# Hybrid decoder trunk on one core: the silu gates of attention, convolution and scan made by ScalarE's Silu function

## What is computed

```python
def hybrid_layer(x, ...):
    h = rms_norm(x, norm_g)
    u = h @ w_in
    c_q, c_kv, k_pe, g_mla, u_conv, g_conv, z, xbc, dt_raw = jnp.split(u, offs, axis=-1)
    o_mla = mla_mixer(c_q, c_kv, k_pe, ...) * jax.nn.silu(g_mla)        # 6 heads x 128
    o_conv = conformer_conv_mixer(u_conv, ...) * jax.nn.silu(g_conv)    # 512 wide, 31 taps, layer norm, silu, @ w_pw
    o_ssd = ssd_mixer(z, xbc, dt_raw, ...)                              # 768 wide, rms_norm(y * silu(z), norm_g)
    y = jnp.concatenate([o_mla, o_conv, o_ssd], axis=-1) @ w_out
    return x + y
```

## Time and profile before

| what | value |
|---|---|
| time, median of 3 runs | 1636.02 us (1632.85 to 1638.46) |
| the profiled execution's own time | 1634.22 us |
| its span, first to last instruction | 1632.4 us |
| TensorE matmul busy | 1555.7 us (95%) |
| VectorE busy | 1066.7 us (65%) |
| ScalarE busy | 615.6 us (38%) |
| mean granted TensorE clock | 0.985 of full speed |
| moved by DMA | 158.13 MB, 97 GB/s |

### The profile page before, as it was taken

How to read it: one execution, slowest core, us unless ns; L and a number is a source line. 1 busy time by engine, 2 the same in 40 slices (tenths; PEclk the granted TensorE clock), 3 DMA queues, 4 the chain that set the end, 5 groups by cost and what they waited for, 6 DMA issues and landing times.

```text
span 1632.4 us, 18535 instructions
## 1 busy us (share of the span) xinstructions
PE 1555.7 (95%) x7062; PEld 1238.4 (76%) x7062; DVE 1066.7 (65%) x1738; ACT 615.6 (38%) x855; POOL 44.6 (3%) x86
## 2 busy tenths in 40 slices
PE   6999999999988999999999999899999799999997
PEld 5877776777776777888877877677778678778886
DVE  6545764889999876543455457758999996773221
ACT  6444453334333344212244355433443334352120
POOL 0000000000000000101000000000000000001100
PEclk9999999999998999999999999999999999999999
DMA  5322221222222323444422223121112233225442
GB/s 214 96 94 78 91 80 63 66 68 73 75 94 84 106 76 100 145 139 155 136 96 75 89 82 100 65 78 65 65 65 98 77 102 102 77 91 167 142 142 65
DMA packets 44423, 158.13 MB, mean 97 GB/s; under 512 B 5520, under 2 KB 5808, under 8 KB 44336
## 3 DMA queue, kind: packets, MB, share of 16 engines
q1 hardware_dynamic: 36720, 129.64, 24.4%
q0 software_dynamic: 6464, 23.12, 5.0%
q10 hardware_dynamic: 1152, 4.19, 0.7%
HBM read 148.50 MB, written 8.44 MB: 96 GB/s over the span
## 4 chain that ended last, share of the span: by engine, by line
PE 69%; DVE 19%; ACT 7%; issue 3%; DMA 1%; DVEq 0%; SPq 0%; POOL 0%; ACTq 0%; POOLq 0%
PE acc L489 14%; PE acc L491 14%; PE acc L490 14%; PE S L489 4%; PE S L490 4%; PE S L491 4%; PE S L494 3%; DVE wlo L986 3%; ACT whi L740 3%; DVE xb L977 3%; DVE cacc L1034 3%; PE T L490 2%; PE T L491 2%; PE T L489 2%; DVE xg L968 1%
## 5 line engine op out<-in xcount | busy, mean ns | idle before, releaser
L489 PE MATMUL acc<-hhi,whi 128*128 128x512 f32 (+1 forms) x1504 | 604.9, 402 | 23.1 <-DVE wlo L986 23.1
L986 DVE TENSOR_TENSOR wlo<-stage,whi 128x1024 fp32r<-128x1024 f32 (+3 forms) x252 | 300.4, 1196 | 451.9 <-ACT whi L740 449.9
L491 PE MATMUL acc<-hhi,wlo 128*128 128x512 f32 (+1 forms) x1504 | 590.5, 393 | 0.0
L490 PE MATMUL acc<-hlo,whi 128*128 128x512 f32 (+1 forms) x1504 | 589.8, 392 | 0.0
L740 ACT ACTIVATE whi<-stage 128x1024 fp32r<-128x1024 f32 (+3 forms) x252 | 259.6, 1035 | 467.3 <-PE acc L491 249.3
L489 PEld LDWEIGHTS acc<-hhi,whi 128*128 128x128 f32 (+1 forms) x1504 | 284.4, 189 | 87.1 <-DVE wlo L986 25.1
L490 PEld LDWEIGHTS acc<-hlo,whi 128*128 128x128 f32 (+1 forms) x1504 | 284.4, 189 | 61.9 <-issue 3.6
L491 PEld LDWEIGHTS acc<-hhi,wlo 128*128 128x128 f32 (+1 forms) x1504 | 283.4, 188 | 62.7
L1034 DVE SCALAR_TENSOR_TENSOR cacc<-glu,pv,cacc 128x512 f32<-128x512 f32 x240 | 171.8, 748 | 4.6
L489 PE MATMUL S<-hhi,whi 128*128 128x512 f32 x192 | 75.5, 393 | 0.0
L728 ACT ACTIVATE prob<-S,cols 128x128 f32<-128x128 f32 (+3 forms) x48 | 25.4, 529 | 131.7 <-DVE cols L972 131.7
(11 more groups left out here) (228 smaller groups left out, 1601.0 us busy)
## 6 DMA issues: line engine op xcount, KB each, us to landing
stage<-weights SPq DMA_DIRECT2D x236, 512.0 KB, 3.4
y_features<-xg POOLq DMA_DIRECT2D x32, 256.0 KB, 4.2
acsb<-acs_rows POOLq DMA_DIRECT2D x16, 384.0 KB, 4.2
xg<-x_features ACTq DMA_DIRECT2D x8, 512.0 KB, 11.4
xr<-x_features POOLq DMA_DIRECT2D x16, 256.0 KB, 4.2
xr<-y_features POOLq DMA_DIRECT2D x16, 256.0 KB, 4.0
stage<-weights SPq DMA_DIRECT2D x8, 256.0 KB, 2.9
stage<-weights SPq DMA_DIRECT2D x4, 384.0 KB, 3.0
```

Of the source, the lines that this page charges most:

```text
L489: nc.tensor.matmul(out, a, c, start=start, stop=False)
L490: nc.tensor.matmul(out, a, d, start=False, stop=False)
L491: return nc.tensor.matmul(out, b, c, start=False, stop=stop)
L986: nc.vector.tensor_tensor(wlo[u % RING][:, 0:w], stage[u % STAGE][:, 0:w], whi[u % RING][:, 0:w].bitcast(F32), ALU.subtract).then_inc(lo_d ...
```

## The change

For gmla, gconv and z, VectorE evicts without the factor 0.5; ScalarE runs Silu on temp and writes the gate itself, into xg for gmla and gconv, into temp2 for z; VectorE's silu() is replaced by gated(), which puts the tap as before and waits for tanh_done, and for z the product reads temp2. ug, xbc and the layer norm's silu stay as they were. The diff:

```diff
@@ -806,8 +806,13 @@
-                        if kind in ("gmla", "ug", "gconv", "z"):
+                        if kind == "ug":
                             tanh()
+                        if kind in ("gmla", "gconv", "z"):
+                            tanhs[0] += 1
+                            gate = temp2[:, :] if kind == "z" else xg[:, i if kind == "gmla" else 6 + i, :]
+                            act.wait_ge(tanh_in.sem, tanh_in.at(layer, tanhs[0]))
+                            a(tanh_done, gate, temp[:, :], ACT.Silu)
@@ -996,6 +1001,13 @@
+                def gated():
+
+                    if taps_open[0]:
+                        convolve(1)
+                    tanhs[0] += 1
+                    dve.wait_ge(tanh_done.sem, tanh_done.at(layer, tanhs[0]))
+
@@ -1142,14 +1154,14 @@
-                            evac(j, temp[:, :], half=True)
+                            evac(j, temp[:, :])
                             mark(tanh_in)
-                            silu(None, xg[:, i if kind == "gmla" else 6 + i, :], temp[:, :])
+                            gated()
                         elif kind == "z":
-                            evac(j, temp[:, :], half=True)
+                            evac(j, temp[:, :])
                             mark(tanh_in)
-                            silu(None, temp[:, :], temp[:, :])
-                            tt(None, xg[:, 10 + i, :], xg[:, 10 + i, :], temp[:, :], ALU.mult)
+                            gated()
+                            tt(None, xg[:, 10 + i, :], xg[:, 10 + i, :], temp2[:, :], ALU.mult)
```

## The result

The changed kernel takes **1627.05 us** (median of 5 runs, 1624.6 to 1629.92) against 1636.02 us (1632.85 to 1638.46): ratio 0.9948, 95% interval 0.9929 to 0.9967. That is 9.0 us less, where 2.9 were forecast; the time lies 1 us under the range. A second, longer comparison (the first experiment) gives 7.6 us. The forecast was right on every term of the path, the chain of work that TensorE waits for, and wrong in pricing TensorE's clock at nothing. What the runs show of the clock is worth about 2 us; the last 2.7 to 4 us of the gain stay open.

The account below looks back on a forecast made before the run. TensorE, busy 95% of the span, was taken as the bound, so only its waits count: 2 layers x 2 gates x 0.72 = -2.9 us, all other terms 0, from 1636.02 to 1633.1 us; range 1628.0 to 1638.8.

Parts of the forecast that it names:

- Removed steps: At 32 gates, one VectorE operation each goes: 22.1 us of VectorE's time, 0.72 us off each chain.
- the four waits: TensorE's waits behind z gates 1 and 5 in both layers, each forecast to shrink by 0.72 us.
- Gates beside TensorE's work, 28 of 32: Gates of gmla and gconv, and z gates 0, 2, 3, 4: TensorE is fully busy there, so no gain.
- Loads ahead of a gate: Table loads of 1.30 us on ScalarE, hidden while it waits at least 1.95 us for the eviction: cost nothing.
- the cover: ScalarE's wait ahead of a gate, 1.95 us at the shortest, hiding a 1.30 us load with 0.65 us left.
- Reloads ahead of the scan's exponentials: Scan steps 5, 6, 7: three exponentials and the weight split behind delayed 1.30 us; cost nothing, bounds 0 to 3.9 us per layer.
- Silu, switches at double cost: Two rivals: Silu takes two passes, 1635.6 us, chance 0.05; table switches cost about double, 1634.6 us, chance 0.10.
- The path's sum, -2.9 us: Two layers times z gates 1 and 5 times 0.72 us, the whole forecast gain.
- The further wait of 0.77 us: TensorE's wait in layer 2 on the same chain as z gate 5, counted with that gate's -0.72 us.
- all other terms 0: Everything but z gates 1 and 5 in the sum, including loads, reloads and the other gates, priced at nothing.
- The rival that came nearest, with -5.2 us: Clock drops around z gates 1 and 5 both go, a further -2.3 us: 1630.8 us, chance 0.13.

Follow-up runs that it names:

- the first experiment: The changed kernel timed again with no edit, beside the kernel before: 1628.82 us against 1636.39, ratio 0.9958.
- The step put back: Changed kernel plus an unread VectorE product where the removed step stood, at z gates 1 and 5: 1634.79 us, 0.999 of the kernel before.
- The extra loads: Changed kernel plus a one-column Silu and Exp, two more table loads, ahead of z gate 1's wait: 1641.56 us, 1.0034 of the kernel before.
- with gate 1 back: Changed kernel plus an unread VectorE product at z gate 1 alone, gate 5 staying short: 1632.69 us, 0.9981 of the kernel before.
- xbc by Silu: Changed kernel plus Silu for the scan inputs, ten tiles per layer: 1639.62 us; with the convolution norm's silu replaced too: 1631.58 us.
- the norm's silu: Changed kernel plus the convolution norm's silu as a ScalarE Silu, with scale and bias in the activation: 1623.54 us, 0.992 of the kernel before.

## Why the prediction was wrong, and where it was right

- **Removed steps:** right. 21.7 us less of VectorE; a step leaves 0.73 us of each of the four waits (0.72). The step put back brings the time back.
- **Gates beside TensorE's work, 28 of 32:** right. Nothing for gmla and gconv (+0.8 us, within the interval), nothing for z gates 0, 2, 3 and 4 (-0.2 us).
- **Loads ahead of a gate:** right: 1.30 us of 1.95. The extra loads show that the cover would have broken at 0.65 us more.
- **Reloads ahead of the scan's exponentials:** right. They take over the wait, cost ScalarE 1.30 us, and TensorE does not see it.
- **Silu, switches at double cost:** both rivals fall by one row each.
- **The path's sum, -2.9 us:** right, as far as the waits go. The further wait of 0.77 us did not shrink, and the sum had nothing from it.
- **The step that failed** is the clock, in "all other terms 0". The sum priced it at nothing, because "after equal waits the drop to 1.2 GHz comes in one layer and not in the other": a lottery with the same odds on both sides. The rival that came nearest, with -5.2 us, was given 0.13. The profiles show that the odds were not the same before and after. At z gate 5 the chain at its old length draws the drop in 12 of 14 cases, and the one layer of the profile read for the forecast that went without it was the rare one; with the step gone it never came (0 of 22). The boundary of the layers, which no rival names, went from 5 of 7 to 2 of 11. The rival was right on gate 5 and not on gate 1, where 1.7 of its 2.3 us lay: there the drop came as often with the short wait as with the long.

How much of the gain that explains: 2.9 us path. A drop behind z gate 5 costs 0.5 to 0.9 us net, since the wait of 0.78 us behind it then does not stand (184.5 to 184.9 us to the layer's end with the drop, 184.0 without, at the same wait for kr); 12 of 14 gone, two layers: 1.1 us or so. The boundary drop costs 72.7 - 71.1 = 1.6 us and went from 5 of 7 to 2 of 11: 0.9 us. Sum 4.9 us of the 7.6 to 9.0 measured, and just the 5.0 us of z gates 1 and 5 alone. For gate 5 alone it gives 1.45 of path and 2.0 of clock, where -2.9 us and, with gate 1 back, -2.5 us were measured.

The mean clock does not close the gap. It rose from 0.9846 to 0.9876, and 0.3% of 1636 us is 4.9 us, which with the path would make 7.8; but only if all of it fell on busy stretches, and behind z gate 5 it does not. Over the 101 executions of the kernel before, a straight line through time and clock gives 0.6 us for each 0.001, with a wide scatter: by that estimate 0.003 is worth 1.8 us.

The traces allow a second count. All 18 hold the same 7062 matmuls in the same order, so every stretch can be timed in each, start to start. Three stretches in which no wait was shortened vary by themselves: the first 50 us of matmuls (49.8 to 52.9), from there to 565 us (500.0 to 503.4) and from 940 to 1330 us (389.8 to 393.0; the places are those of the profile read for the forecast, the two runs with xbc by Silu are left out). The span without these three is 687.6 to 689.5 us, mean 688.7, in the five profiles with both chains long, and 682.6 to 684.4, mean 683.2, in the four of the change and of its z parts with both short. That is 5.6 us, of which some 0.6 are drops behind z gate 1, which fell to the first five by luck: 5.0 us, as by the first count.

The last 2.7 to 4 us are **open**. By both counts they are not at the two gates nor at the boundary. They would have to lie in the three stretches, which together differ by up to 6 us between executions (942.7 to 948.7 us) and in the two groups of profiles by 1.2; whether the change moves the odds there, or the medians of few executions were lucky, no run tells. The 2.4 us at z gate 1 of layer 2 in the first pair of profiles were 0.7 of wait and, for the rest, luck of that pair. And how z gate 5's wait reaches the boundary, 185 us later, is shown by count only, with no cause.

## What to carry to other kernels

Price a removed step by the wait that it shortens, and then look at the granted clock behind that wait: a pause of TensorE that is mostly followed by a drop is worth more than its length, and one or two layers of one profile don't tell how often it comes, so take a second profile of the unchanged kernel before calling it chance. Swap a function for one from another table where ScalarE waits for its operand longer than the load, and where the load comes ahead of that wait. Where the load takes the wait over, it counts in full on ScalarE, and costs time if the reader behind it has no slack: at the scan's exponentials it had some, in attention with xbc by Silu it had none. Before moving on, walk back along the same chain: the next steps of the same kind (here the norm's silu, -13.3 us in all against -7.6) can be worth nearly as much again.

## What was unexpected of the hardware

- Equal instructions and equal waits do not give equal clocks: behind 2.2 us of waiting at z gate 5 the clock fell to 1.2 GHz in 12 of 14 cases, behind 3.1 us at z gate 1 in 3 of 14. The length of the last wait alone does not decide.
- One switch of the table costs 1.28 us and the activation follows within 0.02 us of its end; three switches with two one-column activations took 4.32 us.
- Silu over 128x512 takes 631 ns, as tanh does, and the norm's tanh behind z gate 1's Silu needed no load: both are in one table. The scan's exponentials behind a Silu did need one: exp is not in it.
- Growing a wait by 2.4 us in each layer cost 12.3 us against the change, of which 4.8 are the waits, 4.2 the lower clock right behind them and 1.6 a drop at the boundary of the layers.
